# Seven-product units: VectorE copies the high parts of the three blocks made from weight sums, ScalarE the other four

## The reference

```python
def swiglu(h, w_in, w_out):
    a, b = jnp.split(h @ w_in, 2, axis=-1)
    return (jax.nn.silu(a) * b) @ w_out
...
        h = layer_norm(DN_ALPHA * x + m, ln1_g[i], ln1_b[i])
        f = jnp.square(jax.nn.relu(h @ mlp_w1[i])) @ mlp_w2[i]
        e = jax.nn.sigmoid(h @ ple_w_gate[i]) * (p[i] @ ple_w_proj[i])
        x = layer_norm(DN_ALPHA * h + f + e, ln2_g[i], ln2_b[i])
```

## Time and profile before

| | |
|---|---|
| median of 3 runs | 2668.0 us (2667.74 to 2669.13) |
| profiled execution, its own time | 2670.47 us |
| its span, first to last instruction | 2668.7 us |
| mean granted TensorE clock | 0.994 |
| busy: TensorE, VectorE, ScalarE, GpSimd | 2582.0, 1395.2, 1190.5, 1069.3 us |
| HBM read | 267.09 MB, 101 GB/s |
| seven-product units | 50, of 11.18 us in the steady form |

### The profile page before, as it was taken

The page is one execution under the profiler, slowest core; times in us unless marked ns, Lnnn a source line. Parts: engine busy times, 40 slices in busy tenths (PEclk is TensorE's granted clock), DMA queues, the critical chain, the costliest instruction groups (busy, mean ns, idle before and its releaser), DMA issues.

```text
span 2668.7 us, 40348 instructions
## 1 busy us (share of the span) xinstructions
PE 2582.0 (97%) x15940; PEld 2166.6 (81%) x15940; DVE 1395.2 (52%) x2479; ACT 1190.5 (45%) x2071; POOL 1069.3 (40%) x497
## 2 busy tenths in 40 slices
PE   8999999999999998999999999999999999999998
PEld 6887788887777777898987678889887778888987
DVE  4575543353533357253658857455445565644554
ACT  4454421222533344453543845344345774534543
POOL 2312233434322323464533634455542212554552
PEclk9999999999999999999999999999999999999999
DMA  8623244543222211223232022322331112232332
GB/s 325 230 96 122 83 157 150 182 175 107 75 87 72 72 64 48 92 99 95 92 99 95 17 75 91 95 88 95 111 103 60 44 48 72 87 103 83 100 96 86
DMA packets 49843, 271.62 MB, mean 102 GB/s; under 512 B 5583, under 2 KB 9319, under 8 KB 25608
## 3 DMA queue, kind: packets, MB, share of 16 engines
q1 hardware_dynamic: 45648, 265.71, 29.2%
q10 hardware_dynamic: 4024, 3.54, 0.6%
HBM read 267.09 MB, written 2.13 MB: 101 GB/s over the span
## 4 chain that ended last, share of the span: by engine, by line
PE 62%; issue 24%; DVE 7%; POOL 5%; ACT 3%; POOLq 0%; ACTq 0%; DVEq 0%
PE lin L869 13%; PE lin L871 13%; PE lin L870 13%; PE lin L1949 5%; POOL wlo L754 5%; PE lin L1951 5%; PE lin L1950 5%; DVE bank L3468 2%; PE lin L1421 2%; PE bank L1405 1%; DVE bank L3470 1%; PE bank L1439 1%; PE bank L1600 1%; DVE tlo L3496 1%; ACT ghi L2444 1%
## 5 line engine op out<-in xcount | busy, mean ns | idle before, releaser
L754 POOL TENSOR_TENSOR wlo<-raw,whi 128x1024 fp32r<-128x1024 f32 (+4 forms) x202 | 696.5, 3448 | 1317.5 <-ACT whi L2090 1317.5
L2090 ACT ACTIVATE whi<-raw 128x1024 fp32r<-128x1024 f32 (+4 forms) x202 | 295.4, 1462 | 605.0 <-PE lin L871 542.8
L869 PE MATMUL lin<-hhi,whi 128*128 128x512 f32 x1160 | 466.0, 402 | 6.5 <-issue 2.6
L871 PE MATMUL lin<-hhi,wlo 128*128 128x512 f32 x1160 | 453.7, 391 | 0.0
L870 PE MATMUL lin<-hlo,whi 128*128 128x512 f32 x1160 | 453.0, 391 | 0.0
L869 PE MATMUL lin<-ghi,whi 128*128 128x512 f32 x1136 | 446.5, 393 | 2.9 <-POOL wlo L754 2.1
L871 PE MATMUL lin<-ghi,wlo 128*128 128x512 f32 x1136 | 442.8, 390 | 0.0
L870 PE MATMUL lin<-glo,whi 128*128 128x512 f32 x1136 | 442.8, 390 | 0.0
L775 POOL TENSOR_TENSOR wlo<-raw,whi 128x512 fp32r<-128x512 f32 x200 | 265.1, 1338 | 213.4 <-ACT whi L2422 212.3
L869 PEld LDWEIGHTS lin<-hhi,whi 128*128 128x128 f32 x1160 | 218.6, 188 | 67.4 <-issue 14.9
L1949 PE MATMUL lin<-thi,whi 128*128 128x256 f32 x800 | 230.8, 289 | 33.9 <-ACT lin L2472 27.9
(11 more groups left out here) (537 smaller groups left out, 4408.9 us busy)
## 6 DMA issues: line engine op xcount, KB each, us to landing
raw<-in_w SPq DMA_DIRECT2D x139, 1024.0 KB, 4.9
raw<-in_w SPq DMA_DIRECT2D x85, 512.0 KB, 3.6
adw_a<-in_ada SPq DMA_DIRECT2D x30, 1024.0 KB, 5.0
adw_b<-in_ada SPq DMA_DIRECT2D x18, 1024.0 KB, 5.9
raw<-in_w SPq DMA_DIRECT2D x12, 768.0 KB, 5.5
raw<-in_w SPq DMA_DIRECT2D x8, 640.0 KB, 3.8
raw<-in_w SPq DMA_DIRECT2D x8, 384.0 KB, 3.0
x<-in_x SPq DMA_DIRECT2D x1, 2048.0 KB, 10.0
```

What stands on the lines that cost most here:

```text
L754: nc.gpsimd.tensor_tensor(wlo[:, slot, 0:size], raw[:, slot, 0:size], whi[:, slot, 0:size].bitcast(F32), ALU.subtract).then_inc(s.wlo_ok, 1)
L869: pe.matmul(dst, lh, rh, start=first, stop=False)
L871: return pe.matmul(dst, ll, rh, start=False, stop=last)
L2090: act.activation(whi[:, slot, 0:size], raw[:, slot, 0:size], ACT.Copy).then_inc(s.whi_ok, 1)
```

## The change

VectorE's `block_low` becomes a copy of the sum's bank into `whi` and, behind a wait for that copy, the subtraction. Both count on `blk_lo_v`, 6 per unit in place of 3. ScalarE's `block_high` keeps blocks 0, 3, 4 and 6, `blk_hi` counts 4 per unit in place of 7, and its wait on the sums goes. VectorE now waits itself for the product that frees the block's place, or, at the start of a run, for ScalarE's copy of block 0 or 4, which stands behind what that place was used for before. Nothing else moves, and the arithmetic is the same.

```diff
@@ -770,7 +770,7 @@
                 g = ORDINAL[u]
 
                 def low_block(k, rows, cols, done):
-                    pool.wait_ge(s.blk_hi, HAD["blk_hi"] + 7 * g + k + 1)
+                    pool.wait_ge(s.blk_hi, HAD["blk_hi"] + 4 * g + {0: 1, 3: 2, 4: 3, 6: 4}[k])
                     b = block_at(u, k)
                     nc.gpsimd.tensor_tensor(block_of_four(wlo, b), weight_block(u, rows, cols), block_of_four(whi, b).bitcast(F32),
                                             ALU.subtract).then_inc(done, 1)
@@ -1980,12 +1980,12 @@
                     else:
                         pe.wait_ge(s.a_free, HAD["a_free"] + g)
                     product(0, A, quarter(0, half0), True)
-                    pe.wait_ge(s.blk_lo_v, HAD["blk_lo_v"] + 3 * g + 1)
+                    pe.wait_ge(s.blk_lo_v, HAD["blk_lo_v"] + 6 * g + 2)
                     inputs_ready(0)
                     if u > u0:
                         pe.wait_ge(s.q_free, HAD["q_free"] + g)
                     product(1, Q, combined(0), True)
-                    pe.wait_ge(s.blk_lo_v, HAD["blk_lo_v"] + 3 * g + 2)
+                    pe.wait_ge(s.blk_lo_v, HAD["blk_lo_v"] + 6 * g + 4)
                     inputs_ready(1)
                     pe.wait_ge(s.seed_ok, HAD["seed_ok"] + 2 * g + 1)
                     product(2, U, combined(1))
@@ -1995,7 +1995,7 @@
                     inputs_ready(2)
                     pe.wait_ge(s.seed_ok, HAD["seed_ok"] + 2 * g + 2)
                     product(4, U, combined(2))
-                    pe.wait_ge(s.blk_lo_v, HAD["blk_lo_v"] + 3 * g + 3)
+                    pe.wait_ge(s.blk_lo_v, HAD["blk_lo_v"] + 6 * g + 6)
                     product(5, V, quarter(4, half1))
                     pe.wait_ge(s.wlo_ok, n.up(s.wlo_ok))
                     inputs_ready(3)
@@ -2413,12 +2413,10 @@
                     act.wait_ge(s.prod_mm, HAD["prod_mm"] + 7 * (g - 1) + k + 1)
                 if k == 0:
                     act.wait_ge(s_raw[u % 2], n.up(s_raw[u % 2], 16))
-                if k in (1, 2):
-                    act.wait_ge(s.sum_ok, HAD["sum_ok"] + 3 * g + k + 1)
-                elif k == 4:
+                if k == 4:
                     act.wait_ge(s.dif_ok, HAD["dif_ok"] + g + 1)
-                src = {0: weight_block(u, 0, 0), 1: as_block(B4), 2: as_block(B5), 3: weight_block(u, 1, 0),
-                       4: weight_block(u, 0, 1), 5: as_block(B7), 6: weight_block(u, 1, 1)}[k]
+                src = {0: weight_block(u, 0, 0), 3: weight_block(u, 1, 0), 4: weight_block(u, 0, 1),
+                       6: weight_block(u, 1, 1)}[k]
                 act.activation(block_of_four(whi, b), src, ACT.Copy).then_inc(s.blk_hi, 1)
 
             def combined_high(stage):
@@ -2448,9 +2446,9 @@
 
                     def ahead(*ks):
                         for k in ks:
-                            if more:
+                            if more and k in (0, 3, 4, 6):
                                 block_high(u + 1, k)
-                            elif k == 2 or k == 6:
+                            elif not more and k in (2, 6):
                                 act.wait_ge(s.prod_mm, HAD["prod_mm"] + 7 * g + k)
                                 split((u + 1 + k // 6) % 2, plan[u + 1][1] * plan[u + 1][2])
 
@@ -2503,7 +2501,7 @@
                         st.u += 1
                     if evict is not None:
                         evict(k)
-                    for j in {DC - 2: (0, 1, 2, 3), DC - 1: (4, 5, 6)}.get(k, ()):
+                    for j in {DC - 2: (0, 3), DC - 1: (4, 6)}.get(k, ()):
                         block_high(st.u + (DC - 1 - k), j)
                 tile[0] += DC
 
@@ -2524,10 +2522,10 @@
                 tile[0] += 4
                 silu_pair(tile[0], 0)
                 combined_high(0)
-                for k in range(4):
+                for k in (0, 3):
                     block_high(st.u + 2, k)
                 silu_pair(tile[0], 1)
-                for k in range(4, 7):
+                for k in (4, 6):
                     block_high(st.u + 2, k)
                 st.u += 2
                 tile[0] += 4
@@ -2984,7 +2982,7 @@
                     act.activation(bank, bank, ACT.Sigmoid).then_inc(s.gate_ok, 1)
                     if k == 3:
                         combined_high(1 + i)
-                    for j in {5: (0, 1, 2, 3), 7: (4, 5, 6)}.get(k, ()):
+                    for j in {5: (0, 3), 7: (4, 6)}.get(k, ()):
                         block_high(st.u + 2, j)
                 st.u += 2
                 tile[0] += DC
@@ -3464,7 +3462,7 @@
 
                 g = ORDINAL[u]
                 v.wait_ge(s_raw[u % 2], 16 * (u // 2 + 1))
-                v.wait_ge(s.blk_lo_v, HAD["blk_lo_v"] + 3 * g)
+                v.wait_ge(s.blk_lo_v, HAD["blk_lo_v"] + 6 * g)
                 v.tensor_tensor(as_block(B4), weight_block(u, 0, 1), weight_block(u, 1, 1), ALU.add).then_inc(s.sum_ok, 1)
                 v.wait_ge(s.sum_ok, HAD["sum_ok"] + 3 * g + 1)
                 v.tensor_tensor(as_block(B5), as_block(B4), weight_block(u, 0, 0), ALU.subtract).then_inc(s.sum_ok, 1)
@@ -3474,8 +3472,15 @@
             def block_low(u, k):
 
                 g, b = ORDINAL[u], block_at(u, k)
-                v.wait_ge(s.blk_hi, HAD["blk_hi"] + 7 * g + k + 1)
-                v.tensor_tensor(block_of_four(wlo, b), as_block({1: B4, 2: B5, 5: B7}[k]), block_of_four(whi, b).bitcast(F32),
+                bank, before = {1: (B4, 0), 2: (B5, 2), 5: (B7, 4)}[k]
+                if run_of(u) < u:
+                    v.wait_ge(s.prod_mm, HAD["prod_mm"] + 7 * (g - 1) + k + 1)
+                else:
+                    v.wait_ge(s.blk_hi, HAD["blk_hi"] + 4 * g + (3 if k == 5 else 1))
+                v.wait_ge(s.sum_ok, HAD["sum_ok"] + 3 * g + {1: 1, 2: 2, 5: 3}[k])
+                v.tensor_copy(block_of_four(whi, b), as_block(bank)).then_inc(s.blk_lo_v, 1)
+                v.wait_ge(s.blk_lo_v, HAD["blk_lo_v"] + 6 * g + before + 1)
+                v.tensor_tensor(block_of_four(wlo, b), as_block(bank), block_of_four(whi, b).bitcast(F32),
                                 ALU.subtract).then_inc(s.blk_lo_v, 1)
 
             def combined_sums(stage, src):
```

## The result

The changed kernel takes 2675.66 us, the median of 9 runs, against 2668.0 us for 9 runs of the kernel before: a ratio of 1.0029, 95% interval 1.0018 to 1.0039, or 7.7 us slower. The median is slower by more than the bound of 0.2% (the interval reaches down to 0.18%) and inside the range of 2670 to 2700, but 7.7 us is well under half of the 19 us that were forecast. The profiled execution took 2674.97 us, its span 2673.2 us, 4.5 us over the span of before.

A forecast was written before the change was run, and what follows sets the result against it. TensorE, busy 97%, was taken as the bound, stalling 1.10 us per steady unit ahead of product 4. Terms -0.2 + 7.2 + 3.9 + 4.0 + 3.3 + 1.5 = +19.7 us on 2668.0 gave 2687 us, range 2670 to 2700.

The forecast's parts named there:

- the steady units of the second block: 16 seven-product units within runs: stall of 1.55 us ahead of product 6 against 1.10 before, +7.2 us in all.
- the runs after the gate stage: Two runs: new copies delay a tile eviction that bank U's seed waits for by 1.4 us; 2 x 2.0 = +4.0 us.
- the starts of the middle runs: Six run starts: first sum misses its gap between GpSimd's low parts, 1.1 us later; +0.65 us each, +3.9 us.
- The wait for seed V: TensorE's wait ahead of product 4 for ScalarE's copy seeding bank V: 27.9 us in 31 waits, nearly gone after.
- C22: VectorE's add of P5 to bank U, awaited by product 6; forecast T+9.07 (first block), T+9.54 (second), T being product 0's start.
- the rival of fast copies: VectorE's copies from PSUM run like the SBUF cast, 0.44 us in place of 0.68: no change, 2668 us, chance 0.08.
- The wait of the first sum for GpSimd: VectorE's first sum ends 0.55 us after GpSimd's low part regardless, so block 5's copy costs nothing in steady units.
- Second runs: Second run of each MLP: first sum falls behind another GpSimd low part, product 6 later; 2 x 1.6 = +3.3 us.
- First run: The cold first run: first low part 0.72 us later, a stall near product 6 replaces one of 1.95; +1.5 us.
- the race: VectorE's first sum against GpSimd's low part; rival: the sum starts first, no new stall, near 2657 us, chance 0.09.
- the third rival: The clock falls to half speed in the longer stalls: +30 us, near 2717 us, chance 0.05.
- only the steady units pay: Case in which the run starts add nothing and only units within runs get slower: 2675 us, chance 0.12.

The follow-up runs named there:

- the block 5 kernel: The changed kernel with block 5's copy given back to ScalarE, so that VectorE copies blocks 1 and 2 only: 2671.93 us, ratio 1.0017 to the kernel before.

## Why the prediction was right or wrong

The wait that takes over was forecast rightly; the size was not. Of the 10.4 us by which the sum was too high inside the runs, 4.4 lie in the steady units of the second block, where two steps between VectorE's instructions were too long (+7.2 against +2.8), 3.55 in the runs after the gate stage, where an eviction was forecast late that came no later (+4.0 against +0.45), and 1.8 at the starts of the middle runs.

**The bound, right.** The wait for seed V went, C22 took its place, product 6 is late. The copy from PSUM takes 0.68 us; the rival of fast copies (0.44 us) is out. The wait of the first sum for GpSimd covered block 5's copy in the steady units, as the block 5 kernel shows.

**Steady units, mis-sized.** Forecast +7.0 for both blocks, measured +1.1. Two steps between VectorE's instructions were taken too long:
- The first low part at T+6.41 was taken as VectorE's own pace and given to the first copy. But at 1935.00 before, it had just been let go by ScalarE's copy, which ended at 1934.97 (1934.37 + 0.60), 0.69 us after the start of the third sum, though the row shows no idle time in brackets. VectorE's timeline before:

```profile
1934.31 0.70 DVE L3472 TENSOR_TENSOR bank<-raw,bank 128x512 f32<-128x512 f32 x1
```

Nothing holds the new copy: it comes 0.61 us after the third sum (1936.34 to 1936.95), T+6.34. In the first block it is at T+6.33 (1194.14, T at 1187.81). That is 0.07 to 0.08 us a unit.

- The step from the 256-column product to C22 was taken as 0.47 us, its duration of 0.42 and 0.05 more. No row showed that step free of waits: C22 had waited there for TensorE, 0.28 us in its bracket. Without a wait it follows after 0.33 (1939.60 to 1939.93).

With 0.08 us in the first block C22 is at T+8.99 and not 9.07, with 0.07 + 0.14 in the second at 9.33 and not 9.54; measured are 8.98 (1196.79) and 9.32. The periods then follow, 11.05 and 11.39 within 0.03 us. The rest of the second block's term, 16 x 0.21 = 3.4 against 2.8, is that two of before's units took 11.47 and not 11.18; one of the first block took 11.45, which makes 0.3 of its -1.7.

**Starts of the middle runs, right in mechanism, half in size.** The first sum missed its gap as forecast, 1.63 us in place of 0.70, behind GpSimd's low parts, but C22 gained back the same 0.2 us, and four of the six cost 0.38 us each, the others 0.53 and 0.05.

**The run after the gate stage, wrong.** Forecast 2.0 us each, measured 0.45 for the two. The step that failed is the eviction said to come 1.4 us late. Before, ScalarE sat 7.12 us ahead of block 1's copy, until VectorE's second sum, and the next tile's eviction (line 2984, now 2982) sat behind it. ScalarE's timeline before and after; after's trace stands 1.85 us earlier here (the same evictions ahead of these rows start at 1636.51 and 1634.66):

```profile
1645.43 1.33 ACT L2422 ACTIVATE whi<-bank 128x512 fp32r<-128x512 f32 x2 [7.12 <-DVE bank L3470]
...
1647.17 0.59 ACT L2984 ACTIVATE lin<-lin 128x512 f32<-128x512 f32 x1
```
```profile
1640.78 0.58 ACT L2982 ACTIVATE lin<-lin 128x512 f32<-128x512 f32 x1 [3.80 <-PE lin L871]
```

The eviction is 4.5 us earlier after the offset is taken off. VectorE had stood idle for it, 1.67 us; now it has the tile in hand and puts the new copies where it waited. Its last tile of the stage, which the seed of bank U waits for, starts at 1647.43 against 1649.60, 0.3 us earlier by the same offset. The forecast had put the new work into VectorE's order and had not taken the old wait out of ScalarE's.

**Second runs, right**: +1.46 and +1.45 us against 1.6 each, the length of that unit (10.67 to 12.13 us in the first MLP). Product 6 goes from 1743.83 to 1743.99 only, because the trace of after stood 1.3 us earlier when the unit began:

```profile
1743.99 0.36 PE L1949 MATMUL lin<-thi,whi 128*128 128x256 f32 x1 [1.28 <-DVE lin L3537]
```

**First run, +2.7 against +1.5**, inside its 0 to 4. Product 6 there waits 3.65 us, where product 4 had waited 1.95, and the first unit is 1.7 us longer. The other 0.95 us lie in the second unit, 12.14 us against 11.19, and there the clock has a part that the sum left out: half clock was granted behind the stall in both kernels, before until 1064.5 and after until 1069.7. TensorE in the same stretch, before and then after:

```profile
1067.00:1070.00 3.00, 3.00 (x27) 1.00 0.00 0
```
```profile
1067.00:1070.00 3.00, 3.00 (x18) 0.55 0.00 0
```

**The rivals.** The first sum did not win in the steady units (1.80 us in the first block, 1.33 in the second): the race is lost in every steady unit unless GpSimd is held back, and then it is worth 28 us (2675.66 to 2647.87). In the steady units the clock did not fall behind the new stalls (last section); in the first run it was low for longer, as just shown, which is a small case of the third rival. The case "only the steady units pay" gave 2675, nearly the measured time, and was wrong all the same: most of the loss is at the starts, and the steady units give little.

## What to carry to other kernels

When an engine's wait moves off an in-order queue, ask which single instruction stands ahead of the one that is late: here one copy of three carried the whole gain, 17.5 us, and putting it behind the seed on its own engine gave 34.5 us. Follow a stall to the first link that is longer than the same instruction elsewhere (a sum of 1.80 us where 0.70 is to be had) before moving work between engines. And read an engine's pace only from a pair of rows neither of which had to wait; the absence of a bracket doesn't show that. Before a difference of a few us between two traces is explained by the edit, compare the granted clock of the same stretch in both.

## What the runs showed of the hardware

VectorE's back-to-back intervals were shorter than its durations: 0.61 us for 512 columns, 0.33 for 256 (durations 0.68 and 0.42), and 0.72 where the next one reads the result behind a semaphore (1938.27 to 1938.99).

Of the clock, two stretches of the kernel after, behind the 3.65 us wait of the first run and behind a 1.09 us one in the second block (length, busy time of each engine, then the granted clock, in the third column from the end):

```profile
1064.00:1068.00 4.00, 3.47 (x16) 3.50 (x17) 1.25 (x5) 0.92 (x2) 0.00 (x0) 0.50 0.00 0
1929.00:1933.00 4.00, 3.90 (x32) 3.93 (x33) 2.77 (x6) 2.85 (x7) 0.72 (x1) 1.00 0.00 0
```

Behind 3.65 us of idle it was 0.50, 1.2 GHz; behind 1.09 us it stayed at 1.00, 2.4 GHz, and so it did behind the 1.28 us at 1743.99. The mean of the kernel is 0.996, against 0.994 before.
